# Opening of a two-layer decoder step: two input blocks copied from PSUM by ScalarE, two squares and the first norm's sums placed later

## What is computed

```python
def rmsnorm(x, g):
    y = x * lax.rsqrt(jnp.mean(x * x, axis=-1, keepdims=True) + EPS)
    return y * g
hp = rmsnorm(xp, norm_mix[0])      # xs, the sample tokens, alike
d = hp @ w_down                    # 1024 -> 512 (query) + 256 (latent) + 32 (rope key)
```

## Time and profile before

| | us |
|---|---|
| median of 3 runs | 1959.62 (1959.49 to 1959.9) |
| the profiled execution's own time | 1959.83 |
| its span in the trace | 1958.0 |
| PE busy | 1922.3 (98%) |
| DVE busy | 1073.7 (55%) |
| ACT busy | 758.4 (39%) |
| POOL busy | 702.9 (36%) |

### The profile page before, as it was taken

How to read it: one execution, slowest core, us unless ns; L and a number is a source line. 1 busy time by engine, 2 the same in 40 slices (tenths; PEclk the granted TensorE clock), 3 DMA queues, 4 the chain that set the end, 5 groups by cost and what they waited for, 6 DMA issues and landing times.

```text
span 1958.0 us, 36321 instructions
## 1 busy us (share of the span) xinstructions
PE 1922.3 (98%) x13285; PEld 1845.1 (94%) x13285; DVE 1073.7 (55%) x1844; ACT 758.4 (39%) x1508; POOL 702.9 (36%) x690
## 2 busy tenths in 40 slices
PE   7999999999999999999999999999999999999999
PEld 7886669999999999999999999999889999999998
DVE  3787655565556555468535425428864852542541
ACT  4555555554555555332112112247653211221221
POOL 3340003422223233443333333366545343333331
PEclk9999999999999999999999999999999999999999
DMA  5321001111111110222322322332222222223223
GB/s 148 65 65 36 25 13 43 38 31 50 36 35 34 44 40 16 75 77 85 86 78 84 86 80 81 86 100 73 76 67 83 79 82 86 81 80 86 85 76 91
DMA packets 253078, 131.47 MB, mean 67 GB/s; under 512 B 43073, under 2 KB 250754, under 8 KB 252882
## 3 DMA queue, kind: packets, MB, share of 16 engines
q1 hardware_dynamic: 252514, 128.56, 23.5%
q10 hardware_dynamic: 444, 1.29, 0.2%
HBM read 126.21 MB, written 3.61 MB: 66 GB/s over the span
## 4 chain that ended last, share of the span: by engine, by line
PE 87%; DVE 9%; ACT 2%; issue 2%; DMA 0%; DVEq 0%; POOL 0%; SPq 0%; ACTq 0%; POOLq 0%
PE ps L200 18%; PE ps L203 18%; PE ps L201 18%; PE ps L1220 7%; PE ps L1218 7%; PE ps L1219 7%; PE ps L1248 3%; PE ps L1023 2%; PE ps L998 2%; PE ps L1185 2%; DVE arena L1856 1%; PE ps L232 1%; PE ps L1014 1%; DVE arena L2112 1%; DVE split L1859 1%
## 5 line engine op out<-in xcount | busy, mean ns | idle before, releaser
L200 PE MATMUL ps<-split,whi 128*128 128x288 f32 x3024 | 888.5, 296 | 10.9 <-DVE split L273 4.2
L201 PE MATMUL ps<-split,whi 128*128 128x288 f32 x3024 | 884.8, 295 | 0.0
L203 PE MATMUL ps<-split,wlo 128*128 128x288 f32 x3024 | 855.5, 295 | 0.0
L194 POOL TENSOR_TENSOR wlo<-raw,whi 128x1024 fp32r<-128x1024 f32 x187 | 455.6, 2438 | 614.2 <-ACT whi L171 613.8
L200 PEld LDWEIGHTS ps<-split,whi 128*128 128x128 f32 x3024 | 568.5, 188 | 14.6 <-issue 13.0
L201 PEld LDWEIGHTS ps<-split,whi 128*128 128x128 f32 x3024 | 568.5, 188 | 0.4
L203 PEld LDWEIGHTS ps<-split,wlo 128*128 128x128 f32 x3024 | 555.8, 188 | 0.0
L171 ACT CAST whi<-raw 128x1024 fp32r<-128x1024 f32 x187 | 194.8, 1043 | 373.6 <-DMA raw<-in_ffn_w_up 226.6
L1218 PE MATMUL ps<-split,split 128*128 128x384 f32 x768 | 268.2, 349 | 0.0
L1468 DVE TENSOR_REDUCE ssq<-arena 128x16 f32<-128x1024 f32 x128 | 156.1, 1220 | 186.6 <-ACT arena L1330 186.6
L1220 PE MATMUL ps<-split,split 128*128 128x384 f32 x768 | 257.9, 336 | 0.0
(11 more groups left out here) (282 smaller groups left out, 2095.3 us busy)
## 6 DMA issues: line engine op xcount, KB each, us to landing
raw<-in_ffn_w_up SPq DMA_DIRECT2D x96, 512.0 KB, 3.8
raw<-in_ffn_w_down SPq DMA_DIRECT2D x48, 512.0 KB, 3.9
arena<-in_cache_ckv SPq DMA_DIRECT2D x128, 128.0 KB, 2.0
raw<-in_rec_w_in SPq DMA_DIRECT2D x16, 512.0 KB, 3.9
raw<-in_attn_w_o SPq DMA_DIRECT2D x8, 512.0 KB, 3.9
raw<-in_rec_w_out SPq DMA_DIRECT2D x8, 512.0 KB, 4.1
raw<-in_attn_w_down SPq DMA_DIRECT2D x7, 512.0 KB, 7.6
raw<-in_attn_w_uq SPq DMA_DIRECT2D x48, 64.0 KB, 2.2
```

Source lines behind the costliest of these rows:

```text
L194: pool.tensor_tensor(wlo[:, t % RING, :], raw[:, t % RING, :], f32(whi[:, t % RING, :]), ALU.subtract).then_inc(w_lo, 1)
L200: pe.matmul(o, wh, a, start=first, stop=False)
L201: pe.matmul(o, wh, b, start=False, stop=False)
L203: mm = pe.matmul(o, wl, a, start=False, stop=last)
```

## The change

- ACT now copies input blocks 1 and 3 from PSUM (a new semaphore `xt_ac`), DVE copies 0, 2 and 4.
- ACT's order becomes: square 0, square 1, copy 1, square 2, copy 3, split of tile 0, the eight `norm_high` with the split of tile 1 behind chunk 4 as before, then the split of tile 2, squares 3 and 4, and the root. `down_act` no longer splits tile 2.
- DVE's five `diag` products come behind its eight chunks of `xn_lo`.
- TensorE's `input_sums` moves from behind tile 0 to behind chunk 3 of tile 1; tile 1 therefore takes both halves of the tokens chunk by chunk, as tile 0 does.
- The rotary key's semaphore `kr_n` is dropped, its count goes to `kr_c`. All waits on `xt_ev` count from 3 in place of 5.

```diff
         def input_sums(pe):
-            pe.wait_ge(xt_ev, 3)
+            pe.wait_ge(xt_ev, 2)
...
-        def input_squares(act):
-            for i in range(XTOK):
-                n = P if i < 4 else TN
-                act.wait_ge(s_x[i], 16)
-                if i:
-                    act.wait_ge(x_sq, i)
-                act.activation(sqrow[0:n, :], xin[0:n, i, :], ACT.Square,
-                               accum_out=cols[0:n, 20 + i:21 + i]).then_inc(x_sq, 1)
+        def input_square(act, i):
+            n = P if i < 4 else TN
+            act.wait_ge(s_x[i], 16)
+            if i:
+                act.wait_ge(x_sq, i)
+            act.activation(sqrow[0:n, :], xin[0:n, i, :], ACT.Square,
+                           accum_out=cols[0:n, 20 + i:21 + i]).then_inc(x_sq, 1)
...
+        def keep_input_act(act, i):
+            act.wait_ge(xt_ps, i + 1)
+            act.copy(*input_turned(i)).then_inc(xt_ac, 1)
...
         def keep_inputs(dve):
-            for i in range(XTOK):
-                n = P if i < 4 else TN
+            for i in (0, 2, 4):
                 if i == ROWS_AT:
                     dve.wait_ge(rp_ps, 1)
                     dve.tensor_copy(rpar[:].rearrange("p a b -> p (a b)"), ps[:, 4, 0:DC * R_ALL]).then_inc(rp_ev, 1)
                 dve.wait_ge(xt_ps, i + 1)
...
+                dve.tensor_copy(*input_turned(i)).then_inc(xt_ev, 1)
+            dve.wait_ge(rp_ev, 1)
+            dve.wait_ge(xt_ev, 3)
+            dve.wait_ge(xt_ac, 2)
+            for c in range(DC):
+                norm_chunk_dve(dve, 0, c)
+            for i in range(XTOK):
+                n = P if i < 4 else TN
                 dve.wait_ge(x_sq, i + 1)
                 dve.tensor_scalar(diag[0:n, i, 0:n], ident[0:n, 0:n], cols[0:n, 20 + i:21 + i], None,
                                   ALU.mult).then_inc(x_dg1, 1)
...
         def down_pe(pe):
             pe.wait_ge(rp_ev, 1)
-            pe.wait_ge(xt_ev, XTOK)
+            pe.wait_ge(xt_ev, 3)
+            pe.wait_ge(xt_ac, 2)
             for t in range(7):
-                tile_product(pe, t, t, xn_hi, xn_lo, ready=first_ready(pe) if t == 0 else None).then_inc(w_used, 1)
-                if t == 0:
-                    input_sums(pe)
+                ready = first_ready(pe) if t == 0 else (lambda k: input_sums(pe) if k == 4 else None) if t == 1 else None
+                tile_product(pe, t, t, xn_hi, xn_lo, ready=ready).then_inc(w_used, 1)
...
         def down_act(act):
             for t in range(7):
-                split_hi(act, t + LEAD)
+                if t:
+                    split_hi(act, t + LEAD)
...
             load_rows(act)
-            input_squares(act)
+            input_square(act, 0)
+            input_square(act, 1)
+            keep_input_act(act, 1)
+            input_square(act, 2)
+            keep_input_act(act, 3)
             split_hi(act, 0)
             act.wait_ge(rp_ev, 1)
-            act.wait_ge(xt_ev, XTOK)
+            act.wait_ge(xt_ev, 3)
+            act.wait_ge(xt_ac, 2)
             for c in range(DC):
                 norm_high(act, 0, c)
                 if c == 4:
                     split_hi(act, 1)
+            split_hi(act, 2)
+            input_square(act, 3)
+            input_square(act, 4)
             input_root(act)
             down_act(act)
```

More of the change, by code:

```diff
@@ L385, in input_sums, with input_turned @@
             mm.then_inc(n_ss, 1)
-        def input_squares(act):
-            for i in range(XTOK):
-                n = P if i < 4 else TN
-                act.wait_ge(s_x[i], 16)
-                if i:
-                    act.wait_ge(x_sq, i)
-                act.activation(sqrow[0:n, :], xin[0:n, i, :], ACT.Square,
-                               accum_out=cols[0:n, 20 + i:21 + i]).then_inc(x_sq, 1)
+        def input_square(act, i):
[5 more added lines that the diff above has]
+                           accum_out=cols[0:n, 20 + i:21 + i]).then_inc(x_sq, 1)
+        def input_turned(i):
+            n, b = P if i < 4 else TN, XT_BANK[i]
+            src = ps[:, b:b + 2, :].rearrange("p a (c t) -> p (a c) t", t=P) if i < 4 else \
+                ps[:, b, :].rearrange("p (c t) -> p c t", t=TN)
+            return xT[:, :, i * P:i * P + n], src
+        def keep_input_act(act, i):
+            act.wait_ge(xt_ps, i + 1)
+            act.copy(*input_turned(i)).then_inc(xt_ac, 1)
         def input_root(act):
@@ L416, in keep_inputs @@
                                   ALU.mult).then_inc(x_dg1, 1)
[L417 to L420, removed]
         def keep_gains(dve):
@@ L441, in build @@
         d_f, d_hi, d_lo, d_ch = sem("d_f"), sem("d_hi"), sem("d_lo"), sem("d_ch")
-        kr_n, kr_rot, kr_ok, kr_c = sem("kr_n"), sem("kr_rot"), sem("kr_ok"), sem("kr_c")
+        xt_ac, kr_rot, kr_ok, kr_c = sem("xt_ac"), sem("kr_rot"), sem("kr_ok"), sem("kr_c")
         on_ps, on_ev, s_onat = sem("on_ps"), sem("on_ev"), sem("s_onat")
@@ L490, in key_rotate @@
         def key_rotate(pe):
-            pe.wait_ge(kr_n, 1)
+            pe.wait_ge(kr_c, 1)
             pe.wait_ge(d_ln, 3)
@@ L577, in rope_key @@
             dve.scalar_tensor_tensor(out=krw[0:DR, 1, :], in0=krw[0:DR, 0, :], scalar=smallg[0:DR, G_KR:G_KR + 1],
-                                     in1=krw[0:DR, 3, :], op0=ALU.mult, op1=ALU.mult).then_inc(kr_n, 1)
-            dve.wait_ge(kr_n, 1)
+                                     in1=krw[0:DR, 3, :], op0=ALU.mult, op1=ALU.mult).then_inc(kr_c, 1)
+            dve.wait_ge(kr_c, 1)
             dve.wait_ge(s_cst, 16)
@@ L585, in rope_key_turned @@
             dve.tensor_tensor(two(krw[0:DR, 3, :]), pair(3)[0:DR], two(sinT[0:DR, :]), ALU.mult).then_inc(kr_c, 1)
-            dve.wait_ge(kr_c, 2)
+            dve.wait_ge(kr_c, 3)
             dve.tensor_tensor(krw_rope[:, :], krw[0:DR, 2, :], krw[0:DR, 3, :], ALU.add).then_inc(kr_ok, 1)
@@ L2240, in out_turn @@
             if d == 5:
-                pe.wait_ge(xt_ev, XTOK + 1)
+                pe.wait_ge(xt_ev, 3 + 1)
                 out_block(pe, 4, 0, 4).then_inc(xt_ps, 1)
@@ L2247, in out_turn @@
                     if i % 2 == 0:
-                        pe.wait_ge(xt_ev, XTOK + 2 + i // 2)
+                        pe.wait_ge(xt_ev, 3 + 2 + i // 2)
                     mm = out_block(pe, i, 1, 5 + i // 2, 256 * (i % 2))
@@ L2256, in out_turn @@
                     if i < 4:
-                        pe.wait_ge(xt_ev, XTOK + 5 + i)
+                        pe.wait_ge(xt_ev, 3 + 5 + i)
                     out_block(pe, i, 2, 4 + i if i < 4 else 0).then_inc(xt_ps, 1)
@@ L2281, in out_keep @@
                 act.copy(yn[0:TN, 4, 768:1024], ps[0:TN, 0, 0:256]).then_inc(xt_ev, 1)
-                act.wait_ge(xt_ev, XTOK + 11)
+                act.wait_ge(xt_ev, 3 + 11)
                 act.dma_start(O["y_sample"].rearrange("b t d -> (b t) d")[:, 768:1024], yn[0:TN, 4, 768:1024])\
@@ L2292, in out_store @@
             prompt, sample = O["y_prompt"][0].rearrange("(i p) c -> p i c", p=P), O["y_sample"].rearrange("b t d -> (b t) d")
-            sp.wait_ge(xt_ev, XTOK + 4)
+            sp.wait_ge(xt_ev, 3 + 4)
             sp.dma_start(prompt[:, :, 0:512], yn[:, 0:4, 0:512]).then_inc(s_x[0], 16)
-            sp.wait_ge(xt_ev, XTOK + 5)
+            sp.wait_ge(xt_ev, 3 + 5)
             sp.dma_start(sample[:, 0:512], yn[0:TN, 4, 0:512]).then_inc(s_x[0], 16)
-            sp.wait_ge(xt_ev, XTOK + 7)
+            sp.wait_ge(xt_ev, 3 + 7)
             sp.dma_start(prompt[:, :, 512:768], yn[:, 0:4, 512:768]).then_inc(s_x[0], 16)
-            sp.wait_ge(xt_ev, XTOK + 8)
+            sp.wait_ge(xt_ev, 3 + 8)
             sp.dma_start(sample[:, 512:768], yn[0:TN, 4, 512:768]).then_inc(s_x[0], 16)
             for i in range(4):
-                sp.wait_ge(xt_ev, XTOK + 9 + i // 2) if i % 2 == 0 else sp.wait_ge(y_ev, 1 + i // 2)
+                sp.wait_ge(xt_ev, 3 + 9 + i // 2) if i % 2 == 0 else sp.wait_ge(y_ev, 1 + i // 2)
                 sp.dma_start(prompt[:, i, 768:1024], yn[:, i, 768:1024]).then_inc(s_x[0], 16)
```

## The result

The changed kernel is slower: 1964.66 us median of 16 runs (1962.47 to 1968.63) against 1960.07 (1959.09 to 1963.02, 16 runs), a ratio of 1.0025 with a 95% interval of 1.0018 to 1.0032. The forecast was 1961.5 in a range of 1958.6 to 1963.6, so the sign was right, the size not: +4.6 for +1.8. The profiled execution took 1964.63, its span 1962.7.

A forecast was written before the change was run, and what follows sets the result against it. TensorE, 87% of the chain, was taken to bound the kernel. The start gains 1.1, port holds take 2.9, the rest nothing: 1959.83 + 1.8 = 1961.6, the median 0.2 under it, forecast 1961.5, range 1958.6 to 1963.6.

The forecast's parts named there:

- Step 1 and 2: Opening: first high half at 15.71, 1.08 earlier, and TensorE's start of tile 0 at 17.98, 1.12 earlier.
- Steps 3 to 5: DVE's chunks: turns with POOL's quarters, then holds by tile 1's and tile 2's subtractions; last chunk ends at 28.07.
- the order I had left open: Whether POOL or DVE goes first at 20.1, open by 0.06 us; last chunk within 0.2 us of 28.07 either way.
- the 1.8 of the sum: Tile 0: the start gains 1.1 and the holds take 2.9, in sum +1.8 us.
- Step 6: TensorE in tile 0: clock back at 22.98, two us idle before chunk 5, through at 29.15 against 27.35.
- no fall: TensorE's gap of two us before chunk 5: the clock was taken to stay at its upper level.
- B: Rival: clock falls at about 26.4 in tile 0, +3.2 or +3.6 there, 1962.8 to 1963.3; chance 0.25.
- D: Rival: two stretches of 3.42 us at the lower clock from the gap before chunk 5, +5.2, 1964.8; chance 0.11.
- C: Rival: POOL doesn't get in among DVE's chunks, holds stay as now, tile 0 -0.8, 1958.8; chance 0.13.
- Step 7: Behind tile 0: tile 1's matmuls cost nothing, moved sums the same, about 1.3; tile 2's banks don't wait, 0.8 to spare.

The follow-up runs named there:

- the one with POOL waiting: The changed kernel with POOL's subtraction of tile 2 waiting for DVE's eighth chunk: 1960.89, ratio 1.0007.
- the kernel before with the early split: The kernel before with only the split of tile 2 moved behind the eighth high half, ahead of the root: 1963.91, ratio 1.0015.
- the one that leads by 1.5 at tile 2: The changed kernel with tile 2's split and the sums in their old places, POOL's subtraction of tile 1 waiting for DVE's eighth chunk: 1961.08, ratio 1.0010.
- 6 filling matmuls at the head alone: The changed kernel with 6 identity matmuls into an unused PSUM bank ahead of tile 0: 1965.3 (6 runs), ratio 1.0029.
- the kernel with both remedies: The changed kernel with 6 identity matmuls ahead of tile 0 and POOL's subtraction of tile 2 waiting for DVE's eighth chunk: 1962.05, ratio 1.0010.
- both subtractions waiting: The changed kernel with POOL's subtractions of tile 1 and tile 2 both waiting for DVE's eighth chunk: 1961.31, ratio 1.0002.
- the kernel with 14 filling matmuls: The changed kernel with 14 identity matmuls into an unused PSUM bank ahead of tile 0: 1964.25, ratio 1.0014.

## Why the prediction was wrong

**Step 1 and 2 came out right, step 1 in part by luck.** Copy 3 ran at 13.03 to 14.04 for 13.80 to 14.80; the split then waited 0.55 for its weights (14.58), which the step did not have, and the two about cancel: the first high half came at 15.53 for 15.71, TensorE at 17.87 for 17.98.

**Steps 3 to 5, the port, held to a tenth.** Two subtractions in the chunks, DVE taking turns with the quarters, the last chunk at 28.10 for 28.07. At 20.0 POOL was first, by 0.09, the order I had left open, and again at 22.93; the end of the last chunk did not change by it, as said. What it changed is where TensorE waits: two gaps, at chunks 3 and 4, for one long one at chunk 5. With the clock up and from the same start the port costs 1.9, against the 1.8 of the sum.

**Step 6 failed, in its clock term.** It put the return at "22.98, if at the same moment as now" and took "no fall", so the clock had no price in the sum; it cost 1.4 to 2.1. In the first profile the clock came back at 30.62, in the others at 23.30 and 22.28 with a second fall. The moments differ from one execution to the next also in the kernels that lose nothing there (21.81 in the one with POOL waiting, 22.98 and 23.25 in the kernel before), so a moment read from one trace is no term of a sum. From the first chunk to tile 2 the three profiles take 22.7, 22.2 and 22.1 us, and 20.65 with the clock up. Counted as they stand, the openings are 4.0, 3.8 and 3.2 late.

**The reason given for no fall doesn't hold either.** The prediction weighed two places of one trace, one with a fall and one without, and found its case nearer the second, at 1439 us. In 17 profiles, that same place had a fall in five, each worth 1.4 to 1.6 us. Here it is in the kernel with the split of tile 2 back (windows):

```profile
1439.94:1443.36 3.42, 0.51 (x4) 0.54 (x5) 3.25 (x7) 2.19 (x3) 0.00 (x0) 1.00 0.00 0
1443.36:1446.77 3.41, 3.41 (x16) 3.41 (x16) 0.02 (x1) 0.10 (x1) 2.36 (x1) 0.50 0.00 0
```

The other place, at 1419 us, had no fall in two of the 17. So neither outcome belongs to a place.

**The rivals.** B was the right mechanism in the second and third profile (+3.2 to +3.6 forecast, +3.8 and +3.2 measured). D comes near the first profile, by a longer time at the lower level in the same gaps. Its size, 1964.8 for a median of 1964.66, is partly luck: it put +5.2 into the opening, which has 4.0. It had 0.11. The mistake behind both weights was to take two gaps in one trace, one with a fall and one without, as a reason to expect none. C is out: POOL got in both times.

**Step 7** costed the moved sums at nothing, which is right for the whole change (no wait ahead of tile 2) and right only because of the moved split: 1.9 without it. The root needed 37.45 + 0.76 - 34.54 = 3.67 from the sums' start, as reckoned.

**What is left.** Of +4.6 in the median, 3.2 to 4.0 are in the opening. Up to 960 us the three profiles of the changed kernel then lose 0.4, 0.0 and 0.0 more against the first profile of before. Behind 960 us, without the falls at 1443 us, all 14 profiles of the changed kernel and of those built on it lose another 0.3 to 0.8, in small steps, the clearest near 1385 and between 1570 and 1600 us. The second profile of before and the kernel before with the early split lose 0.1 to 0.2 there. So this part may come with the change; no run was made for it, and its cause stays open. What decides in which executions the clock falls at 166, 1419 or 1443 us stays open too. No kernel was measured to beat the kernel before; the one that leads by 1.5 at tile 2 has a median 0.9 above it.

## What to carry to other kernels

An idle engine is not a free place. A split on ACT that waited for nothing released a POOL instruction of 2.4 us in front of DVE's critical chunks, so follow what a moved step's result sets off, and ask which port that needs at that moment. Where TensorE waits in small gaps at the head of a kernel, price them twice, as they stand and with the clock at its lower level behind them; with 6 filling matmuls at the head alone the fall moved into the gaps and nothing was gained. And where the times of a kernel fall in groups, compare means or groups as well as medians, and look in the trace for what a group has lost.

## What the runs showed of the hardware

**Who starts first has the port for the whole instruction, and hundredths decide it.** At 955 us DVE's last low half and a POOL subtraction are asked at nearly the same time. In the first profile of the kernel before DVE is first, in the second POOL (timelines):

```profile
954.47 0.76 DVE L1860 TENSOR_TENSOR split<-arena,split 128x576 f32 x1
...
955.08 2.41 POOL L194 TENSOR_TENSOR wlo<-raw,whi 128x1024 fp32r<-128x1024 f32 x1 [1.97 <-ACT whi L171]
```

```profile
954.83 2.88 DVE L1860 TENSOR_TENSOR split<-arena,split 128x576 f32 x1
...
954.75 2.34 POOL L194 TENSOR_TENSOR wlo<-raw,whi 128x1024 fp32r<-128x1024 f32 x1 [1.28 <-ACT whi L171]
```

The windows of that second profile:

```profile
955.08:958.50 3.42, 0.86 (x6) 0.73 (x6) 2.63 (x1) 0.00 (x0) 2.02 (x1) 1.00 0.00 0
958.50:961.92 3.42, 3.42 (x17) 3.42 (x16) 0.75 (x1) 0.00 (x0) 0.00 (x0) 0.50 0.41 107
```

POOL first by 0.08, and the same program is 2.2 later there, and 4.0 once the clock has fallen behind the gap. In the 17 profiles of this study, of 14 kernels, POOL was first in three (at 956.18 in the kernel with both remedies, at 955.45 with both subtractions waiting, and this one), by 0.03 to 0.21, and the kernel was 2.2 to 3.7 later behind it each time. It is the opening's mechanism, port and then clock, at a place that the change does not touch. It makes this execution's 4 us; how much of the kernel's spread from 1959.09 to 1963.02 it makes, no trace shows.

**A DVE product with one tensor input waits for the port too**: the five `diag` products, each 128x128 from SBUF to SBUF, took 3.24 for 1.02 beside a POOL subtraction.

**The clock's moments are not the program's.** In five traces of two kernels it comes back first at 22.98 and 23.25 (before), at 30.62, 23.30 and 22.28 (changed). A gap of 1.8 us at the upper level in tile 0 left the clock up in the kernel with 14 filling matmuls; in the one with 6 and POOL waiting the clock fell within such a gap, at 23.09.
